# mLSTM chunk loop: old numerators turned before the next scores and keys, gated output before weights and statistics

## The reference

```python
def mlstm_chunk(carry, inp):
    C, n, m = carry
    q, k, v, ig, lf = inp
    ...
    D = jnp.where(causal, Fh[:, :, :, None] - Fh[:, :, None, :] + igh[:, :, None, :], NEG)
    ...
    S = jnp.einsum('bthd,bshd->bhts', q, k) * jnp.exp(D - m_t[..., None])
    inter = jnp.exp(a - m_t)
    num = jnp.einsum('bhts,bshd->bthd', S, v) + inter.transpose(0, 2, 1)[..., None] * jnp.einsum('bthk,bhkv->bthv', q, C)
    ...
    C_new = decay[..., None, None] * C + jnp.einsum('bhs,bshk,bshv->bhkv', ws, k, v)
```

## Time and profile before

| | us |
|---|---|
| median of 3 runs | 2194.12 |
| lowest and highest of them | 2191.2, 2201.19 |
| the profiled execution's own time | 2199.8 |
| its span | 2197.8 |
| TensorE busy in the span | 2024.2 |
| VectorE, ScalarE, GpSimd busy | 1045.1, 761.8, 525.7 |
| the chunk loop with its sample part, first matmul to last copy | about 392.6 to 508.6 |

### The profile page before, as it was taken

The page is one execution under the profiler, slowest core; times in us unless marked ns, Lnnn a source line. Parts: engine busy times, 40 slices in busy tenths (PEclk is TensorE's granted clock), DMA queues, the critical chain, the costliest instruction groups (busy, mean ns, idle before and its releaser), DMA issues. The chain is left out here.

```text
span 2197.8 us, 33297 instructions
## 1 busy us (share of the span) xinstructions
PE 2024.2 (92%) x13868; PEld 1873.2 (85%) x13868; DVE 1045.1 (48%) x1761; ACT 761.8 (35%) x1432; POOL 525.7 (24%) x440
## 2 busy tenths in 40 slices
PE   6999999876888986998899999899999999999997
PEld 6999999865666763565799989899999999999997
DVE  6888762456887873214232243533333323322222
ACT  4323323534766761212322232322222224432212
POOL 2444321204654562222011112111111001211000
PEclk9999999876999987999999999999999999999998
DMA  6455431101000006454433331323333333332332
GB/s 206 138 172 174 157 119 32 40 6 39 1 1 20 1 1 225 123 165 134 154 92 92 93 97 44 96 87 90 94 88 87 95 106 92 105 104 87 87 90 66
DMA packets 258148, 203.12 MB, mean 92 GB/s; under 512 B 20342, under 2 KB 237276, under 8 KB 252687
## 3 DMA queue, kind: packets, MB, share of 16 engines
q1 hardware_dynamic: 246399, 150.92, 23.6%
q0 software_dynamic: 6144, 39.46, 5.3%
q10 hardware_dynamic: 5456, 10.62, 1.5%
HBM read 178.59 MB, written 26.54 MB: 93 GB/s over the span
## 5 line engine op out<-in xcount | busy, mean ns | idle before, releaser
L2997 DVE TENSOR_TENSOR ffn_w_l<-ffn_raw,ffn_w_h 128x1024 fp32r<-128x1024 f32 (+1 forms) x136 | 163.9, 1206 | 273.7 <-ACT ffn_w_h L2930 273.4
L98 PE MATMUL banks<-h_h,ffn_w_l 128*128 128x264 f32 x1408 | 287.2, 285 | 5.5 <-DVE ffn_w_l L2997 5.5
L98 PE MATMUL banks<-h_h,ffn_w_h 128*128 128x264 f32 x1408 | 288.2, 286 | 0.0
L98 PE MATMUL banks<-h_l,ffn_w_h 128*128 128x264 f32 x1408 | 287.2, 285 | 0.0
L2930 ACT CAST ffn_w_h<-ffn_raw 128x1024 fp32r<-128x1024 f32 (+1 forms) x136 | 138.6, 1021 | 331.5 <-PE banks L98 330.4
L98 PEld LDWEIGHTS banks<-h_h,ffn_w_l 128*128 128x128 f32 x1408 | 220.4, 189 | 6.0 <-DVE ffn_w_l L2997 5.8
L98 PEld LDWEIGHTS banks<-h_h,ffn_w_h 128*128 128x128 f32 x1408 | 219.4, 189 | 0.0
L98 PEld LDWEIGHTS banks<-h_l,ffn_w_h 128*128 128x128 f32 x1408 | 218.8, 189 | 0.0
L2918 POOL TENSOR_TENSOR act_l_rest<-ffn_act,act_h 128x528 fp32r<-128x528 f32 x38 | 71.5, 1883 | 375.8 <-ACT act_h L2938 375.8
L89 PE MATMUL banks<-fm_hT_h,fm_w_l 128*128 128x352 f32 x648 | 147.3, 336 | 1.4 <-DVE hT_l L918 1.4
L680 POOL TENSOR_TENSOR fm_w_l<-fm_raw,fm_w_h 128x512 fp32r<-128x512 f32 x54 | 95.1, 1762 | 220.8 <-ACT fm_w_h L754 220.7
(11 more groups left out here) (522 smaller groups left out, 4264.9 us busy)
## 6 DMA issues: line engine op xcount, KB each, us to landing
ffn_raw<-in_w_ffn_in_dram SPq DMA_DIRECT2D x88, 512.0 KB, 3.8
ffn_raw<-in_w_ffn_out_dram SPq DMA_DIRECT2D x32, 512.0 KB, 4.0
fm_raw<-in_w_in_dram SPq DMA_DIRECT2D x44, 256.0 KB, 3.1
early_w_raw<-in_w_in_dram SPq DMA_DIRECT2D x32, 256.0 KB, 3.0
merge_raw<-in_w_in_dram SPq DMA_DIRECT2D x32, 256.0 KB, 2.9
ffn_raw<-in_w_ffn_out_dram SPq DMA_DIRECT2D x16, 384.0 KB, 3.5
hT_copy<-fm_hT_h SPq DMA_DIRECT2D x4, 1056.0 KB, 5.3
hT_copy<-hT_l SPq DMA_DIRECT2D x4, 1056.0 KB, 5.3
```

Source lines behind the costliest of these rows:

```text
L98: mm = pe.matmul(out[:, bank, 0:cols.stop - cols.start], w[:, kt, :], x[:, cols], start=(first and n == 0), stop=(last and n == 2))
L2997: dve.tensor_tensor(w_l[n % NSPLIT][:, 0:m, :], raw[n % NRAW][:, 0:m, :], w_h[n % NSPLIT][:, 0:m, :].bitcast(F32), ALU.subtract).then_inc( ...
```

## The change

TensorE's `ahead` is split in two. `broadcasts(c + 1)` stays at the head of body c. `scores_and_keys(c + 1)` now stands behind the wait for the state of chunk c - 1 (`s_c`, for every c from 1 to 7) and, from chunk 5 on, behind `turn_out(c - 5)` with its wait for `s_hn`. On VectorE `gated_output(c - 5)` moves from behind the statistics to a place between the scaled queries and the weights; in chunk 8, which has no weights, it stands ahead of the statistics of chunk 7. No instruction is added or removed, and ScalarE's, GpSimd's and SyncE's programs stay as they are.

```diff
-            def ahead(c):
+            def broadcasts(c):
...
                 mm.then_inc(s_bc, 1)
+
+            def scores_and_keys(c):
+                n, t = tokens(c)
                 if c:
                     pe.wait_ge(s_wt, c)
...
-            ahead(0)
+            broadcasts(0)
+            scores_and_keys(0)
             for c in range(S + 1):
                 n, t = tokens(c)
                 if c < S:
-                    ahead(c + 1)
+                    broadcasts(c + 1)
                 if c:
                     pe.wait_ge(s_c, MH * c)
                 if c >= BACK:
                     turn_out(c - BACK, DC + 1)
+                if c < S:
+                    scores_and_keys(c + 1)
...
                 if c < S:
                     scaled_queries(c + 1)
+                if c >= BACK:
+                    gated_output(c - BACK, DC + 1)
+                if c < S:
                     weights(c + 1)
                 if c:
                     statistics(c - 1)
                 if c == S // 2:
                     scale_and_shift(0)
-                if c >= BACK:
-                    gated_output(c - BACK, DC + 1)
```

## The result

| | before | after |
|---|---|---|
| median, us (5 runs each) | 2198.86 | 2207.38 |
| lowest and highest | 2191.2, 2201.19 | 2206.01, 2208.86 |
| ratio, 95% interval | | 1.0043, 1.0028 to 1.0057 |
| profiled execution's span | 2197.8 | 2207.0 |
| TensorE busy | 2024.2 | 2024.6 |

The change costs 9.5 us by the ratio (6.2 to 12.5), within the 0.5% that I had called no change, and clear of the measurement's own uncertainty. 2201.3 was forecast, which is 2194.12 + 7.2; five runs put the median before at 2198.86 instead of 2194.12, and 4.74 of the 6.1 us by which the forecast is low come from that.

A forecast was written before the change was run, and what follows sets the result against it. TensorE, busy 2024.2 of 2197.8 us, was taken as the bound, with only the mLSTM stage's end shifting. The terms summed to +7.2 us on a median of 2194.12, giving 2201.3 us, slower by 0.33%; range 2194.5 to 2209.5.

The forecast's parts named there:

- chunk 4, state wait: TensorE, chunk 4: scores now wait for VectorE's late state and start later, passed on whole, +1.05 us.
- chunk 5, displaced work and clock: TensorE, chunk 5: scores and keys move behind the turned heads, partly at the low clock, +1.23 us.
- chunk 6, displaced work: TensorE, chunk 6: scores and turned keys now stand behind the turned heads, ahead of the numerators, +1.43 us.
- clock in chunks 6 and 7: TensorE: longer waits bring one more low-clock stretch, taken in chunk 6, +1.5 us; bounds -1.5 and +6.5.
- chunk 7, displaced work: TensorE, chunk 7: scores and keys of the 32 sample tokens leave the wait's cover, +0.99 us.
- chunk 8, VectorE: VectorE, chunk 8: gated output ahead of statistics must first wait for the turned heads, +1.01 us.
- bound of 1.10: Upper bound for the delay of chunk 4's scores by the state wait; lower bound 0.05 us.
- Gain 0: VectorE, chunks 5 to 7: earlier gated output frees `s_at` earlier, but it was never late, so 0 us.
- Rival A: Clock stays low into chunk 8's sample numerators: shift 19 us, 2213 us, slower by over 0.5%; chance 0.08.
- one of two: TensorE's short gaps: the trace showed the low clock after only one of two, 1.65 but not 1.72 us.
- B: Moved scores stay covered by slack behind the turned heads in chunks 6 and 7: +3.3 us, 2197.4; chance 0.12.
- C: The change gains, with a lucky clock and chunks 4 and 8 absorbed: 0 to -1 us, 2193.5; chance 0.05.

The follow-up runs named there:

- e5_null: Kernel before with seven empty lines added to its source, same instructions: loop 99.28 us, device time 1.0016 of before.
- filling: Whole change, with scores and turned keys issued once more ahead of the waits in chunks 5 to 7: chunk 6 9.53 us, loop 104.64.
- e11: Whole change, with scores issued twice and turned keys once more ahead of the waits in chunks 5 to 7: chunk 7 9.81 us, loop 103.15.
- e2_dve_only: Kernel before with only VectorE's new order, TensorE's order as before: loop 99.50 us, device time 1.0026 of before.
- e3_from5: Whole change, but in chunks 1 to 4 the scores stand ahead of the state wait as before: loop 105.27 us, device time 1.0061 of before.
- e12_stats_first: Whole change, but in chunk 8 VectorE does the statistics ahead of the gated output, as before: loop 107.40 us, one run only.
- e7_swap: Kernel before, with each sample's state product ahead of the turned heads in the sample part: loop 88.23 us, device time 0.9949 of before.
- e6_after_again: The whole change once more, unaltered: loop 107.75 us, device time 1.0045 of before.
- e1_pe_only: Whole change with VectorE's order put back as before, so TensorE's new order alone: loop 107.15 us, device time 1.0045 of before.
- e8_late_swap: Kernel before with the sample-part swap, and turned heads behind the numerators in chunks 5 to 7: loop 86.52 us, device time 0.9948 of before.

## Why the prediction was right

It was made as a sum of terms, and each has its measurement now (first run of the change against before, then its repetition against the null):

| term | forecast | measured |
|---|---|---|
| chunk 4, state wait | 1.05 | 1.06, 1.05 |
| chunk 5, displaced work and clock | 1.23 | 1.00, 1.29 |
| chunk 6, displaced work | 1.43 | 1.34 (filling) |
| clock in chunks 6 and 7 | 1.5 | 1.09, 2.80 |
| chunk 7, displaced work | 0.99 | 0.92 (full clock, e11 less e2) |
| chunk 8, VectorE | 1.01 | 1.02, 1.07 |
| sum | 7.2 | 6.43, 8.47 |

*What bounds the kernel.* The forecast said that the shift of the stage's end is all. Against before, the loop's +6.43 and +7.90 (107.75 - 99.85) carry most of the measured 9.5 and 9.9 us; the remaining 3.1 and 2.0 us are of the size of the null's own offset, and I don't explain them. The stages behind kept their length within their scatter. That 2207.38 lies 2 us inside the stated range's upper end is owed to this offset and to the low median at the start, not to a term of the sum.

*Chunks 1 to 4.* Right in mechanism and size: e3_from5 took it away. Its bound of 1.10 was too low, since e12_stats_first paid 2.69 in the same place: the clock can be low in chunk 4 too, a case that I had not given a price.

*Chunk 5.* Right in size, and the two pairs of the table are kinder than the scatter: the four kernels with TensorE's old order (before, e5_null, e2_dve_only, e7_swap) have 12.58 to 13.39, the four with the change's order and gated output (the change, e6_after_again, e3_from5, e12_stats_first) 13.87 to 14.47. The means differ by 1.22, single pairs by 0.5 to 1.9. "Gain 0" for the early gated output was right only against the old order. With the scores behind the turned heads it saves about 0.8 us (e1_pe_only), which my 1.23 contained without saying so, since I had the state products start unhindered.

*Chunks 6 and 7, displaced work.* 1.34 for 1.43, and 9.81 - 8.89 = 0.92 for 0.99, both separated from the clock by runs at full clock.

*Clock.* In chunk 6 the low clock cost 10.87 - 9.53 = 1.34 and 12.35 - 9.53 = 2.82 us; the 1.5 that I took from one stretch in chunk 7 is near the first and half of the second. That chunk 6 would run low was a guess from one stretch of each kind, and its size changes from run to run, so that the sum of 7.2 lies between the two runs is partly luck. In chunk 7 it had been paid before (10.47 - 8.89 = 1.58) and was paid again (11.14 - 9.81 = 1.33, and 1.64): -0.25 and -0.02. Rival A wanted it to reach the samples; each sample head still takes 1.95 us, so it did not. The Trainium skill (TensorE: Matmul & The Clock Gate, "Why this matters for your kernels") says that an idle gap can send the engine back to its half clock. From that I had made an estimate of 4 to 6 us, with every lengthened gap paid for; measured are 1.1 and 2.8, since chunks 5 and 7 were low before as well. My count of "one of two" short gaps left out chunk 8's 1.42 us, behind which the clock was full.

*Chunk 8.* Right, by e12_stats_first and e2_dve_only.

*Rivals.* B (covered) is out: the columns of chunks 6 and 7 move by their work. C (gain) is out.

## What to carry to other kernels

Work that an engine does while it waits is free until it is put behind the wait: before moving an instruction past one, look whether its idle time ended there, and count what is moved at its full length, and the idle time that grows ahead of it as a risk for TensorE's clock. Two engines that take turns show as equal idle times in a timeline (2.84 us here, three times): a product stood behind a wait that it didn't need, and swapping two groups of matmuls gave 11 us there, more than this change moved. And read a short stage by its own length: with seven empty lines the whole program's time came out 3.5 us higher (0.4 to 6.8).

## What the runs showed of the hardware

The clock behind a short idle time is not settled by that idle time. Behind 2.16 us or more it was low at least for a part of the stretch in all 12 cases (chunks 6 and 7 of six runs); behind 1.72 and 1.73 in chunk 6 it was full in all six; behind 1.65 and 1.66 in chunk 7 it was low in five of six; behind 0.98 in chunk 4 it was low once in eight. In chunk 7 of e8_late_swap it fell with 0.49 us as the longest idle time since chunk 5's wait (busy us of PE, PEld, DVE, ACT, POOL, then the clock):

```profile
454.82:458.18 3.36, 3.36 (x17) 3.36 (x18) 1.51 (x10) 1.41 (x4) 0.68 (x4) 0.54 0.00 0
```

What else decides, the traces don't show. The Trainium skill (TensorE: Matmul & The Clock Gate, "The HAM clock gate") says that how many matmuls run cold at a kernel's start differs between runs of one kernel. The two runs of the change show the same in the middle of a kernel: 5.92 and 7.39 us for the same work behind the same 3.25 us.
